# Hybrid encoder trunk: the dilated layer's keys kept in four runs, and GpSimd's rotary, sum, copy and weighting work given to VectorE and ScalarE

## The reference

```python
B_GROUPS = ((128, 1), (512, 4), (2048, 16))        # (window, dilation)

def mixer_b(q, k, v, pos):
    q, k = apply_rope(q, pos), apply_rope(k, pos)
    outs, lses = [], []
    for g, (window, dil) in enumerate(B_GROUPS):
        qg = q[:, g * MIX_HEADS:(g + 1) * MIX_HEADS]
        o, lse = band_attention(dilate(qg, dil)[..., None, :, :], dilate(k, dil), dilate(v, dil),
                                window // (2 * dil), return_lse=True)
        outs.append(undilate(o[..., 0, :, :], dil)); lses.append(undilate_rows(lse[..., 0, :], dil))
    wts = jax.nn.softmax(jnp.stack(lses), axis=0)
    return jnp.einsum('gbhl,gbhld->bhld', wts, jnp.stack(outs))
```

## Time and profile before

| | |
|---|---|
| median of 3 runs | 2321.35 us (2320.59 to 2321.8) |
| the profiled execution | 2322.24 us, its span 2320.4 us |
| TensorE (PE) matmul busy | 2190.5 us, 94% of the span |
| VectorE (DVE) busy | 1591.6 us, 69% |
| ScalarE (ACT) busy | 1125.3 us, 48% |
| GpSimd (POOL) busy | 613.8 us, 26% |
| chain that ended last | TensorE 74%, VectorE 18%, issue 4%, ScalarE 2% |
| layer 0's pairs / output projection | about 108 to 716 us / to 885 us |
| layer 1's pairs / output projection | about 914 to 2183 us / to the end |

### The profile page before, as it was taken

How to read it: one execution, slowest core, us unless ns; L and a number is a source line. 1 busy time by engine, 2 the same in 40 slices (tenths; PEclk the granted TensorE clock), 3 DMA queues, 4 the chain that set the end, 5 groups by cost and what they waited for, 6 DMA issues and landing times.

```text
span 2320.4 us, 32404 instructions
## 1 busy us (share of the span) xinstructions
PE 2190.5 (94%) x11072; PEld 1820.8 (78%) x11072; DVE 1591.6 (69%) x3285; ACT 1125.3 (48%) x2697; POOL 613.8 (26%) x465
## 2 busy tenths in 40 slices
PE   8999999999999978999999999999999999999996
PEld 8877777878887767787787877877878778788875
DVE  7677777777653768567767777677677776666375
ACT  5454544445543333454555645645546456465332
POOL 0313132221000212333442443343424433200021
PEclk9999999999999988999999999999999999999998
DMA  8211111111237441112112112122121121214743
GB/s 263 82 46 46 55 46 51 46 60 37 64 122 243 128 140 55 42 43 63 58 47 73 52 60 70 39 61 64 47 73 52 60 69 38 87 51 150 231 137 131
DMA packets 206797, 190.35 MB, mean 82 GB/s; under 512 B 20132, under 2 KB 160492, under 8 KB 206636
## 3 DMA queue, kind: packets, MB, share of 16 engines
q1 hardware_dynamic: 206636, 188.29, 26.1%
HBM read 160.01 MB, written 28.23 MB: 81 GB/s over the span
## 4 chain that ended last, share of the span: by engine, by line
PE 74%; DVE 18%; issue 4%; ACT 2%; DMA 1%; POOL 0%; SPq 0%; DVEq 0%; ACTq 0%
PE bank L1093 13%; PE bank L1095 13%; PE bank L1094 13%; PE bank L1143 8%; PE bank L1169 7%; DVE work L1544 6%; PE bank L1157 4%; PE bank L1263 4%; PE bank L1269 4%; PE bank L1267 4%; DVE ring L1544 3%; PE bank L1133 2%; DVE work L1646 1%; DVE sums L1544 1%; ACT ring L1309 1%
## 5 line engine op out<-in xcount | busy, mean ns | idle before, releaser
L1093 PE MATMUL bank<-x_ops,ring 128*128 128x512 f32 (+1 forms) x1808 | 857.8, 474 | 43.4 <-DVE work L1617 26.5
L1095 PE MATMUL bank<-x_ops,ring 128*128 128x512 f32 (+1 forms) x1808 | 704.3, 390 | 0.0
L1094 PE MATMUL bank<-x_ops,ring 128*128 128x512 f32 (+1 forms) x1808 | 701.4, 388 | 0.0
L1544 DVE SCALAR_TENSOR_TENSOR ring<-raw,ring 128x512 fp32r<-128x512 f32 x400 | 309.9, 777 | 390.8 <-ACT ring L1309 389.4
L1093 PEld LDWEIGHTS bank<-x_ops,ring 128*128 128x128 f32 x1808 | 348.3, 193 | 108.9 <-issue 51.2
L992 POOL TENSOR_TENSOR work<-work,trig 32x512 f32<-32x512 f32 (+3 forms) x152 | 200.1, 1322 | 811.2 <-DVE work L1631 731.5
L1095 PEld LDWEIGHTS bank<-x_ops,ring 128*128 128x128 f32 x1808 | 344.2, 190 | 71.9
L1094 PEld LDWEIGHTS bank<-x_ops,ring 128*128 128x128 f32 x1808 | 349.3, 193 | 64.7 <-issue 20.9
L1370 ACT COPY work<-bank 128x256 f32<-128x256 f32 (+2 forms) x448 | 164.7, 368 | 458.4 <-PE bank L1157 458.2
L1309 ACT CAST ring<-raw 128x512 fp32r<-128x512 f32 x400 | 248.0, 622 | 201.3 <-PE bank L1269 173.8
L1143 PE MATMUL bank<-work 128*128 128x256 f32 (+2 forms) x896 | 309.5, 428 | 32.3 <-DVE soft L1663 32.3
(11 more groups left out here) (77 smaller groups left out, 2493.6 us busy)
## 6 DMA issues: line engine op xcount, KB each, us to landing
raw<-in_w_in_b SPq DMA_DIRECT2D x160, 256.0 KB, 3.0
raw<-in_w_out SPq DMA_DIRECT2D x128, 256.0 KB, 2.9
raw<-in_w_in_a SPq DMA_DIRECT2D x80, 256.0 KB, 3.0
work<-weight_scratch SPq DMA_DIRECT2D x24, 768.0 KB, 5.0
y_scratch<-work SPq DMA_DIRECT2D x32, 512.0 KB, 2.7
x_ops<-y_scratch SPq DMA_DIRECT2D x64, 256.0 KB, 3.7
raw<-in_w_mkv SPq DMA_DIRECT2D x32, 256.0 KB, 5.2
work<-in_x SPq DMA_DIRECT2D x4, 1024.0 KB, 8.3
```

The costliest lines, as they stand in the source:

```text
L1093: nc.tensor.matmul(dst, w_h, x_h, start=start, stop=False, skip_group_check=again)
L1094: nc.tensor.matmul(dst, w_h, x_l, start=False, stop=False, skip_group_check=again)
L1095: return nc.tensor.matmul(dst, w_l, x_h, start=False, stop=stop, skip_group_check=again)
L1544: return nc.vector.scalar_tensor_tensor(out=dst, in0=a, scalar=1.0, in1=b, op0=ALU.mult, op1=op)
```

## The change

The keys of layer 1 are stored in four runs (`order=4`). Group 1's scores then read a run of keys contiguously, group 0's read four runs of 64 keys, so that its scores come out in another order, which `mask` undoes while it reads them. The copy into 16 runs goes from GpSimd (step 6) to ScalarE (step 23), and reads with a stride of 4. The cosine and sine multiplications, `fourth_sum` and the third weighting go from GpSimd to VectorE. A rotation's four operations now stand in four steps that follow each other, and the second half of a pair's rotations starts earlier. GpSimd keeps only the small work of the layer norms, half of their additions and a few memsets. In the diff, lines without a sign that are not code say where a piece stands.

```diff
 class Pair
-            self.ropes = [(0, 1, 17, 23), (0, 0, 25, 32)]
+            self.ropes = [(0, 1, 17), (0, 0, 25)]
...
-            self.ropes = [(0, 1, 17, 23), (1, 1, 24, 30), (0, 0, 31, 37), (1, 0, 38, 44)]
+            self.ropes = [(0, 1, 17), (1, 1, 21), (0, 0, 25), (1, 0, 29)]
...
-            add_pair(w_in_b[0], B_K + i * DH, Dest(b_k, "k"), B_V + i * DH, Dest(b_v, "v"))
+            add_pair(w_in_b[0], B_K + i * DH, Dest(b_k, "k", order=4), B_V + i * DH, Dest(b_v, "v"))
...
         def b_tiles(g):
             q, tiles = b_q[g], []
+            kd = b_k.rearrange("p (r n) -> p r n", r=4)
             if g == 0:
                 for t in range(TILES - 1):
-                    tiles.append((q[:, t * P:(t + 1) * P], b_k[:, t * P:(t + 2) * P], 2 * P, m_b,
+                    tiles.append((q[:, t * P:(t + 1) * P], kd[:, :, 32 * t:32 * t + 64], 2 * P, m_b,
                                   [(t, 0), (t + 1, P)]))
-                ends = b_k.rearrange("p (t n) -> p t n", n=P)[:, 0:TILES:TILES - 1, :]
+                ends = b_k.rearrange("p (r t n) -> p r t n", r=4, t=TILES)[:, :, 0:TILES:TILES - 1, :]
...
-                qd, kd = dilated(q, 4), dilated(b_k, 4)
+                qd = dilated(q, 4)
 SyncE, exchange, step 29
-                        sp.wait_ge(mixed, 8 * i + 2)
-                        sp.wait_ge(comb_pool, 2 * i + 1)
+                        sp.wait_ge(mixed, 10 * i + 3)
                         load_weights(1)
 GpSimd: fourth_sum (L977 to 985), rotate (L987 to 997), keys_in_runs (L999 to 1005), mix (L1007
 to 1011) and their calls in the program are taken out
 ScalarE
+            def keys_in_runs(i):
+                act.wait_ge(*ready(FIRST_PAIR[1] + 3 * i + 1, 0, 0))
+                nc.scalar.copy(b_k16.rearrange("p (a b m) -> p a b m", a=4, b=4),
+                               b_k.rearrange("p (b m a) -> p a b m", a=4, b=4)
+                               ).then_inc(k16_done, 1)
...
+                            if T == step_at(1, 3 * i + 2, 23):
+                                keys_in_runs(i)
 VectorE
             def first_sum(g):
                 if g > 0:
                     dve.wait_ge(w_lo, stage_of(g - 1, 2) + 1)
-                    dve.wait_ge(s4_done, g)
...
+            def fourth_sum(g):
+                if g > 0:
+                    dve.wait_ge(w_lo, stage_of(g - 1, 3) + 1)
+                dve.wait_ge(s2_done, g + 1)
+                two(sums[:, 1], quarter(g, 3), sums[:, 0], ALU.subtract).then_inc(s4_done, 1)
...
+            def by_cosine(key):
+                g, e, h = key
+                dve.wait_ge(rope_turned, rope_no[key] + 1)
+                for view, take in pairs[g].dests[e].views(h, ROPE):
+                    two(view, view, take(cosb[:, h * HALF:(h + 1) * HALF]), ALU.mult)
+
+            def by_sine(key):
+                g, e, h = key
+                for b, take in turned_views(pairs[g].dests[e], h):
+                    mul = two(b, b, take(sinb[:, h * HALF:(h + 1) * HALF]), ALU.mult)
+                mul.then_inc(rope_mul, 1)
 mask, group 0 of layer 1
+                s, raw_s = s_view(layer, count % 3, size), SB[count % 2][:, 0:size]
+                if layer == 1 and job.group == 0 and not job.whole:
+                    raw_s = raw_s.rearrange("p (r n) -> p n r", r=4)
+                    s, m = (v.rearrange("p (n r) -> p n r", r=4) for v in (s, m))
 mix: parts 0, 1 and 2 are now the three products by the weights, parts 3 and 4 the two additions
+                if part < 3:
...
+                    two(o[part], o[part], wT[:, part, :], ALU.mult).then_inc(mixed, 1)
 VectorE, run
+                    pair = pair_at(layer, T, 23)
+                    if pair is not None and pair.g + 1 < FIRST_PAIR[layer] + PAIRS[layer]:
+                        fourth_sum(pair.g + 1)
...
-                    if T in rope_ends_at[layer]:
-                        turn_ends(rope_ends_at[layer][T])
-                    if T in ropes_at[layer]:
-                        turn(ropes_at[layer][T])
+                    for part, rotary in enumerate((turn, by_cosine, by_sine, turn_ends)):
+                        if T - part in ropes_at[layer]:
+                            rotary(ropes_at[layer][T - part])
...
                             for h, first in ((0, 26), (1, 35)):
-                                if first <= s < first + 4:
+                                if first <= s < first + 5:
                                     mix(i, h, s - first)
 VectorE, memory_projection (end)          VectorE, out_projection (before the last norms)
+                fourth_sum(0)                +                    fourth_sum(FIRST_PAIR[1])
```

More of the change, by code:

```diff
@@ L420, in steps @@
             return range(STEPS * PAIRS[layer] + TAIL)
-        rope_no, gate_no, tanh_no = {}, {}, {}
-        ropes_at, rope_ends_at, tanh_at, gates_at = ([{}, {}] for _ in range(4))
+        rope_no, gate_no = {}, {}
+        ropes_at, tanh_at, gates_at = ([{}, {}] for _ in range(3))
         for layer in range(DEPTH):
@@ L427, in encoder @@
                 T0 = step_at(layer, g - FIRST_PAIR[layer], 0)
-                for e, h, turn, end in pairs[g].ropes:
-                    ropes_at[layer][T0 + turn] = rope_ends_at[layer][T0 + end] = (g, e, h)
+                for e, h, turn in pairs[g].ropes:
+                    ropes_at[layer][T0 + turn] = (g, e, h)
                     rope_no[g, e, h] = len(rope_no)
@@ L975, in _ @@
             pool.wait_ge(consts, 4)
-            def fourth_sum(g):
-                load = load_of(g, 3)
-                pool.wait_ge(s2_done, g + 1)
-                pool.wait_ge(raw_in[load % RAW], landed_value(load))
-                if g > 0:
-                    pool.wait_ge(w_lo, stage_of(g - 1, 3) + 1)
-                nc.gpsimd.tensor_tensor(sums[:, 1], raw[:, load % RAW], sums[:, 0], ALU.subtract
-                                        ).then_inc(s4_done, 1)
-            def rotate(key):
-                g, e, h = key
-                dest = pairs[g].dests[e]
-                pool.wait_ge(rope_turned, rope_no[key] + 1)
-                for view, take in dest.views(h, ROPE):
-                    nc.gpsimd.tensor_tensor(view, view, take(cosb[:, h * HALF:(h + 1) * HALF]),
-                                            ALU.mult)
-                for view, take in turned_views(dest, h):
-                    mul = nc.gpsimd.tensor_tensor(view, view, take(sinb[:, h * HALF:(h + 1) * HALF]),
-                                                  ALU.mult)
-                mul.then_inc(rope_mul, 1)
-            def keys_in_runs(i):
-                pool.wait_ge(*ready(FIRST_PAIR[1] + 3 * i + 1, 0, 0))
-                if i > 0:
-                    pool.wait_ge(s_ready, tile_count(jobs[1][3 * i - 1], TILES - 1) + 1)
-                nc.gpsimd.tensor_copy(b_k16.rearrange("p (r n) -> p r n", r=16), dilated(b_k, 16)
-                                      ).then_inc(k16_done, 1)
-            def mix(i, h):
-                pool.wait_ge(weight_in, 16 * (2 * i + h + 1))
-                pool.wait_ge(o_free, 2 * jobs[1][3 * i + 2].number + 2)
-                o = b_o[2][:, h * HALF:(h + 1) * HALF]
-                nc.gpsimd.tensor_tensor(o, o, wT[:, 2, :], ALU.mult).then_inc(comb_pool, 1)
             def run(layer):
@@ L1015, in run @@
                     if layer == 1:
-                        for i in range(HEADS):
-                            s = T - step_at(1, 3 * i + 5, 0)
-                            if s in (26, 35):
-                                mix(i, (s - 26) // 9)
-                            if T == step_at(1, 3 * i + 2, 6):
-                                keys_in_runs(i)
                         if T == step_at(1, 37, 0):
@@ L1024, in run @@
                             nc.gpsimd.memset(m_b, 0.0).then_inc(zeroed, 1)
-                    pair = pair_at(layer, T, 23)
-                    if pair is not None and pair.g + 1 < FIRST_PAIR[layer] + PAIRS[layer]:
-                        fourth_sum(pair.g + 1)
-                    if T in ropes_at[layer]:
-                        rotate(ropes_at[layer][T])
             def norms(layer):
@@ L1662, in mask @@
                 start = 3.0e38 if job.sink is None else sinks_neg[:, job.sink:job.sink + 1]
-                nc.vector.tensor_tensor_reduce(s_view(layer, count % 3, size),
-                                               SB[count % 2][:, 0:size], m, 1.0, start, ALU.add,
-                                               ALU.min, low[:, job.stat, t:t + 1]
-                                               ).then_inc(s_free, 1)
+                s, raw_s = s_view(layer, count % 3, size), SB[count % 2][:, 0:size]
+                if layer == 1 and job.group == 0 and not job.whole:
+                    raw_s = raw_s.rearrange("p (r n) -> p n r", r=4)
+                    s, m = (v.rearrange("p (n r) -> p n r", r=4) for v in (s, m))
+                nc.vector.tensor_tensor_reduce(s, raw_s, m, 1.0, start, ALU.add, ALU.min,
```

(4 more changed lines are left out.)

28 lines of the change are left out of this document (10 added, 18 removed).

## The result

The changed kernel takes 2272.26 us (median of 4 runs, 2270.71 to 2274.23) against 2321.57 for the kernel before on the same chip: a ratio of 0.9787, 95% interval 0.9775 to 0.9799. It is 49 us faster where 74 were forecast, and 0.26 us above the top of the range. The profiled execution took 2270.71 us, with a span of 2268.9.

A forecast was written before the change was run, and what follows sets the result against it. TensorE was taken to wait for VectorE, slowed beside GpSimd. 2322.2 - 43 (keys) - 22 (layer 0) - 8 (layer 1's stalls) - 2 (first head) + 1 (added fourth sums) = 2248 us; range 2208 to 2272.

The forecast's parts named there:

- What bounds it: TensorE's matmuls fill 94% of the span; its repeated waits in both layers all end on VectorE, slowed beside GpSimd.
- Keys in runs: Group 1's score tiles in layer 1: contiguous keys save 0.45 us a tile, 43 us (23 to 46).
- The second rival: The stride of the queries sets group 1's slow tile: only 0.24 us a tile saved, 2267 us; chance 0.13.
- Layer 0: TensorE's waits for the normalisation and for `summed` both go: 22 us saved, less 3 for what stays already taken off.
- Layer 1, third pair: The 1.44 us wait goes; ScalarE and VectorE tie at step 26; third score tile stalls 2.5 us instead of 3.10.
- third rival: Strided reads are slow on VectorE too, cosine and sine for group 2 queries: 12 us, 2260 us; chance 0.09.
- Layer 1, first pair: Four rotations between steps 17 and 32 bring new TensorE waits of 0.6 us at `summed` and 0.7 at the mask.
- First head, 2 us: In layer 1's first head the 2.7 us wait becomes the 0.7 of a first pair, 2 us saved.
- Clock, 0: Layer 1's clock loss of about 22 us stays, as a 2.5 us stall is nearer to 2.94 than to 1.28.
- The first rival: The third score tile's stall shortens enough for the clock to stay up: 2212 us; chance 0.20.
- The fourth rival: VectorE's long operations are not GpSimd's doing; 21 added a head cost up to 1.78 us each: about 2370; chance 0.04.
- three signs of being wrong: Group 1's tiles keep 1.1 us; third-tile wait gone or beyond 3.5 us; ScalarE's key copy holds step 26's low part.

The follow-up runs named there:

- rot_late: The changed kernel with the two rotations of the group 1 queries moved from steps 21 and 29 of the first pair to 33 and 37: 2248.58 us.
- mix_late: The changed kernel with the combination of the branches later, first half at step 31 instead of 26, second at 37 instead of 35: 2234.83 us.
- tables_q: The changed kernel with cosine and sine of the group 2 queries read from the tables without a stride, products not the reference's: 2250.59 us.
- tables_all: The changed kernel with cosine and sine of the group 2 queries and of the keys read without a stride: 2250.77 us.
- copy_early: The changed kernel with ScalarE's copy of the keys into 16 runs at step 15 of the third pair instead of step 23: 2277.07 us.

## Why the prediction was right or wrong

**What bounds it**: right. Nearly every wait was VectorE's order: moving its operations took TensorE's waits for VectorE in layer 1 from 52 us to under 6.

**The step that failed**: the count of VectorE's chains in layer 1. In the third pair cosine and sine stand at 0.61 us each and take 1.0 where their tables are read with a stride; in the first pair 0.6 and 0.7 us of new waits were counted and 1.0 each measured; the wait of 0.4 at the end of the second pair was put at nothing.

**Keys in runs, 43 us**: right. A tile saves 0.46 us at the upper clock (0.45 taken), and by the earlier trace rows's distance the 96 tiles took 113.7 us and take 72.1: 41.6 saved. What is missing to 44 lies in the stretch of the lower clock, which the term did not consider. Group 0's tiles, costed at nothing, take 63.8 us together and took 63.5. The second rival (the queries' stride) is refuted: 0.68 us with the stride in place.

**Layer 0, 22 us**: 18.4 measured. The waits for `summed` nearly went; the one for the normalisation (L1109), 0.4 us in 9 tiles, stayed. With 0.16 us for each of the 12 waits left, 6.1 us stayed where 3 had been taken off.

**Layer 1, third pair**: the wait of 1.44 us went (1.3 measured), and ScalarE's copy is a tie, as said. "12 operations [...]: 7.3 us" is what failed: from the low part at 1214.56 to the first mask at 1222.52 they take 7.96 us. Without the stride the stall was 2.36 us, the value forecast; with it 2.97. That is the third rival, priced at 12 us with a chance of 0.09. The price was sound in its sum (0.6 us a head at the third tile, 0.1 at the end of the third pair, 0.4 at the end of the second pair, which the rival had left out), the clock aside. The chance was too low, and by a misread row. The 248 ns of the copies with 128 elements are the mean of three kinds. Their shortest, median and longest, in ns, are:

```profile
L1689 DVE COPY trig<-trig x36: 217/258/272, 1037.8 to 2066.5; 16x128 f32<-16x128 f32 x36
```

The 12 copies without a stride take 217 to 219 ns, the 24 with strides of 4 and 16 elements 256 to 272. The trace of the kernel before already showed that a stride slows VectorE; the mean hid it.

**Layer 1, first pair**: the two new waits were forecast at 0.6 and 0.7 us and measured at 1.0 each, counted from matmul to matmul with what follows them. From the low part at 1239.51 to the end of `summed` at 1247.09 + 0.73 = 1247.82 it was 8.31 us instead of 8.05. An operation at 0.61 was right. The shuffles were counted too low: the one at 1243.31 starts 0.1 to 0.2 us behind the addition that it follows. `rot_late` shows that the moved rotations make both waits; how the 0.7 us beyond the count divides was not measured. In all a head of layer 1 was forecast to keep 3.8 of 4.5 us of stalls and kept 5.6: 1.8 us a head, 20 us of the miss of 25.

**First head, 2 us**: the stall of 2.7 us at its second pair went, but its first pair got one of 2.2 us: the x_ops conversions (4.87 us on VectorE) stand in front of the first rotation there.

**Clock, 0**: wrong in our favour, 8 us. The stall kept its length, and yet the clock stayed up in 3 of 11 heads. Nothing in the prediction foresaw this; it was luck, and it hid part of the miss. The first rival's mechanism is sound all the same: behind no stall the clock stays up (`mix_late`).

**The fourth rival** is refuted. `first_sum` takes 0.69 us without GpSimd beside it, and VectorE's busy time rose by 38 us, where at most 120 were forecast.

**The signs**: none of the three signs of being wrong came (tiles at 0.68, the wait at 2.97 us, no wait for the key copy). They did not cover the step that failed. What told was the sign on the other side: VectorE's two-input operations were not at 0.68 throughout.

**Range**: the terms of the waits, "good to about 1 us a head", gave 11 us; the case of the third rival together with somewhat longer waits ended at 2272, and the median is 2272.26. The two should have been added, not stood side by side.

## What to carry to other kernels

When work moves onto an engine, price each operation by the access pattern that it will have there. A row of the same shape without the stride is not a price, and the mean of a group that mixes patterns isn't one either: ask for its shortest and longest. Count the chain up to the next mask that another engine waits for, and look first at what in it could run later: moving 18 operations a head by up to 12 steps brought 69 us, more than the change itself. An engine that holds up one kind of another's operations is still of use beside operations of the other kinds: one sum a pair on GpSimd brought 15 us more.

## What the runs showed of the hardware

- VectorE's two-input operation on 32x512 fp32 takes 0.67 us with contiguous inputs, and 1.03 to 1.06 with one SBUF input at a stride of 4 or of 16 elements. Reading PSUM with these strides (`summed`) costs nothing: 0.67 to 0.69. For SBUF this is as the Trainium skill's page SBUF — State Buffer, section Door 1: The DMA port swizzle, has it for accesses that each reach a new 16-byte line; a stride of 4 elements, 16 bytes, already pays in full here.
- TensorE's score tile with 256 moving columns, by the earlier trace rows's distance: at the fourth tile 1.14 us with the columns at a stride of 4 and 0.68 without at the upper clock, 1.32 and 1.28 at the lower; at the third, behind the stall, 1.35 and 0.91 at the upper, 1.50 and 1.47 at the lower.
- GpSimd's 128x512 operation takes 1.29 us alone, and while it runs VectorE's operations with two SBUF inputs stand still: two of 1.27 together took 2.37.
- The clock behind a stall: the lower level followed 11 of 11 stalls of 4.2 us (from matmul to matmul), 10 of 11 with 3.6, 7, 8, 10 and 11 of 11 in the four kernels with 3.3 to 3.4, 3 and 6 of 11 with 2.8, 5 of 11 with 2.4, none with 0.4 or 0.6. Longer stalls had it more often, but the length alone does not decide: it cost 5 us between two kernels with equal stalls (`tables_q`, `tables_all`), and executions of one program, 8 us apart, had granted clocks of 0.984 and 0.979 (`copy_early`). What decides a single case stays open.
